# Delta rule's triangular inverse: transpose by 128x128 TensorE transposes and a ScalarE copy

## The reference

```python
lower = jnp.where(strict, jnp.einsum("nbhid,nbhjd->nbhij", kb, kc) * decay, 0.0)
eye = jnp.eye(c, dtype=F32)
rhs = jnp.concatenate([vc * bc[..., None], kb * jnp.exp(gc)[..., None]], axis=-1)
sol = lax.linalg.triangular_solve(lower + eye, rhs, left_side=True, lower=True)
```

## Time and profile before

| what | us |
|---|---|
| median of 3 runs | 1694.83 |
| lowest and highest | 1693.57 and 1696.85 |
| profiled execution, span | 1692.8 |
| PE busy | 1670.1 |
| DVE busy | 1152.0 |
| ACT busy | 968.3 |

### The profile page before, as it was taken

One profiled execution on the slowest core, in us unless ns is written; L12 is line 12 of the kernel. 1 busy time (PEld: TensorE's weight loads), 2 busy tenths in 40 slices (PEclk: granted clock), 3 DMA queues, 4 the chain that ended last, 5 costly groups with the idle time before them and its releaser, 6 DMA issues.

```text
span 1692.8 us, 24538 instructions
## 1 busy us (share of the span) xinstructions
PE 1670.1 (99%) x10066; PEld 1383.8 (82%) x10066; DVE 1152.0 (68%) x1835; ACT 968.3 (57%) x1522; POOL 19.9 (1%) x54
## 2 busy tenths in 40 slices
PE   9999999999999999999999999999999999999998
PEld 7778888887888888888888888888888888888886
DVE  6887875778788667555676578655575556985554
ACT  7845554577374447444667676544464456975443
POOL 1000000010000000000000000000000000000000
PEclk9999999999999999999999999999999999999999
DMA  7323355542244555455544335555555555455553
GB/s 265 125 82 132 147 183 187 178 169 107 77 168 162 180 196 188 178 195 177 210 185 153 134 124 177 218 194 190 208 192 194 181 217 187 149 187 180 193 180 143
DMA packets 41872, 291.67 MB, mean 172 GB/s; under 512 B 4673, under 2 KB 4929, under 8 KB 7713
## 3 DMA queue, kind: packets, MB, share of 16 engines
q1 hardware_dynamic: 39312, 280.68, 46.0%
q0 software_dynamic: 2304, 8.91, 1.5%
q10 hardware_dynamic: 144, 0.52, 0.1%
HBM read 289.05 MB, written 1.05 MB: 171 GB/s over the span
## 4 chain that ended last, share of the span: by engine, by line
PE 84%; DVE 10%; ACT 3%; issue 1%; DMA 1%; SPq 0%; DVEq 0%; ACTq 0%
PE pg L535 21%; PE pg L538 21%; PE pg L536 21%; PE pg L485 4%; PE pg L487 3%; PE pg L486 3%; DVE wl L2004 3%; PE ps L843 2%; PE ps L678 2%; DMA raw<-weights 1%; ACT wh L1339 1%; PE ps L892 1%; PE ps L662 1%; PE ps L964 0%; DVE hTl L2603 0%
## 5 line engine op out<-in xcount | busy, mean ns | idle before, releaser
L2004 DVE TENSOR_TENSOR wl<-raw,wh 128x1024 fp32r<-128x1024 f32 x494 | 581.3, 1220 | 183.7 <-ACT wh L1339 180.6
L535 PE MATMUL pg<-wh,hTh 128*128 128x512 f32 x1676 | 661.0, 394 | 1.3 <-ACT arena L1391 1.0
L538 PE MATMUL pg<-wh,hTl 128*128 128x512 f32 x1676 | 653.4, 390 | 0.0
L536 PE MATMUL pg<-wl,hTh 128*128 128x512 f32 x1676 | 652.5, 389 | 0.0
L1339 ACT ACTIVATE wh<-raw 128x1024 fp32r<-128x1024 f32 x522 | 522.8, 1054 | 201.7 <-DMA raw<-weights 191.4
L538 PEld LDWEIGHTS pg<-wh,hTl 128*128 128x128 f32 x1676 | 314.5, 188 | 67.0 <-DVE hTl L2070 0.3
L535 PEld LDWEIGHTS pg<-wh,hTh 128*128 128x128 f32 x1676 | 314.8, 188 | 64.0 <-ACT arena L1391 1.4
L536 PEld LDWEIGHTS pg<-wl,hTh 128*128 128x128 f32 x1676 | 315.0, 188 | 62.2
L485 PE MATMUL pg<-wh,hTh 128*128 128x512 f32 x416 | 171.4, 412 | 2.2 <-DVE wl L2004 2.2
L1445 ACT ACTIVATE arena<-pg,sm 128x256 f32<-128x256 f32 (+1 forms) x67 | 36.6, 547 | 237.4 <-PE pg L538 237.3
L487 PE MATMUL pg<-wh,hTl 128*128 128x512 f32 x416 | 163.0, 392 | 0.0
(11 more groups left out here) (406 smaller groups left out, 1322.7 us busy)
## 6 DMA issues: line engine op xcount, KB each, us to landing
raw<-weights SPq DMA_DIRECT2D x265, 1024.0 KB, 4.8
arena<-wide POOLq DMA_DIRECT2D x9, 512.0 KB, 3.7
raw<-weights SPq DMA_DIRECT2D x2, 512.0 KB, 6.4
cst<-const_tables POOLq DMA_DIRECT2D x1, 1024.0 KB, 5.3
plainh<-dist_tables POOLq DMA_DIRECT2D x2, 512.0 KB, 6.2
arena<-gate_mix POOLq DMA_DIRECT2D x1, 1024.0 KB, 8.3
x<-x_in ACTq DMA_DIRECT2D x1, 512.0 KB, 3.9
x<-x_in SPq DMA_DIRECT2D x1, 512.0 KB, 9.5
```

The source lines that it names most:

```text
L535: pe.matmul(dst, high, wh[:, slot, at], start=start, stop=False)
L536: pe.matmul(dst, high, wl[:, slot, at], start=False, stop=False)
L538: return pe.matmul(dst, low, wh[:, slot, at], start=False, stop=stop)
L2004: tt(wl[:, slot, h], raw[:, slot, h], wh[:, slot, h], ALU.subtract)\
```

## The change

Products are still 64x64, but the transpose of X is no longer updated beside X. In each level PE does the first block, then transposes all of X with eight full 128x128 transposes into banks 2 and 3, then `prepare(1)`; ACT copies the 128x1024 result to `XT_` (a new wait `inv_w` on ACT and `inv_w_read` on PE); PE then does one block of 32 products for X's new term. A 128x128 transpose of a pair of chunks also swaps which row half a chunk's block lies in, so all products now run between the two row halves, in quarters (0,0), (1,1), (1,0), (0,1), and the bank goes by the half that is read. The third block, DVE's addition to the transpose (L2292), the copy to `LT`, the second transposes at L858, the separate start of `XT_` (L2261, L2268, L2270) and ACT's copies at the end (L1559) go. The last level is like the others. DVE writes all finished matrices with eight additions of 64x256 after one wait, two of them before `inv_scaled`'s first signal and six before its second. The masks of a level become 128 wide: the constants hold 5 masks of 64 and 6 of 128 columns instead of 12 of 64, 320 columns more in the same DMA.

```diff
-MASK_NAMES = ("eye", "up", "lo", "ups", "los", "nlo1", "nlo2", "nlo4", "nlo8", "nlo16", "nlo32", "nup1")
+MASK_NAMES = ("eye", "up", "lo", "ups", "los")
+STEPS = (1, 2, 4, 8, 16, 32)
...
-    for s in (1, 2, 4, 8, 16, 32):
-        c[f"nlo{s}"] = -1.0 * ((q // (2 * s) == g // (2 * s)) & (q // s > g // s))
-    c["nup1"] = -1.0 * ((q // 2 == g // 2) & (q < g))
-    main = np.concatenate([np.asarray(c[n], np.float32) for n in CONST_NAMES + MASK_NAMES], 1)
+    for s in STEPS:
+        same_pair = q // (2 * s) == g // (2 * s)
+        c[f"step{s}"] = np.concatenate([-1.0 * (same_pair & (q // s < g // s)), -1.0 * (same_pair & (q // s > g // s))], 1)
+    names = CONST_NAMES + MASK_NAMES + tuple(f"step{s}" for s in STEPS)
...
+        STEP_MASK = {s: cst[:, at + i * P:at + (i + 1) * P] for i, s in enumerate(STEPS)}
+        at += len(STEPS) * P
...
+        def halves(ap, last=False):
+            return ap.rearrange("p (q m f) -> p q m f" if last else "p (m q f) -> p m q f", m=M, f=CHUNK)
...
-                L4, LT4, X4, XT4, T4 = (blocks(v) for v in (Lm, LT, X_, XT_, TM_))
+                L4 = blocks(Lm)
+                inverse, turned, term = halves(X_, True), halves(XT_, True), halves(TM_)
...
-                def natural(v):
-                    return lambda d, h, m, a: v[a, 4 * d + h, m, :]
-                def paired(v):
-                    return lambda d, h, m, a: v[a, 4 * (h // 2) + 2 * d + h % 2, m, :]
-                def block_products(bank, ds, lhs, rhs, from_home, to_home, done, move=None):
-                    for d in ds:
-                        for h in range(2):
-                            for m in range(M):
-                                for g in range(2):
-                                    for r in range(2):
-                                        a, b = (half(r if home or not g else 1 - r) for home in (from_home, to_home))
-                                        at, i = (2 * d + h) * M + m, (d, 2 * g + h, m, a)
-                                        out_ = ps[b, bank + g, at * CHUNK:(at + 1) * CHUNK]
-                                        if move and g:
-                                            pe.matmul(out_, ident[a, a], move(*i), start=True, stop=False)
-                                        last = pe.matmul(out_, lhs(*i), rhs(*i), start=not (move and g), stop=True)
-                    last.then_inc(sem[done], 1)
+                def place(q):
+                    return slice(q * CHUNK, (q + 1) * CHUNK)
...
-                                last = pe.matmul(ps[half(r), d, (h * M + m) * CHUNK:(h * M + m + 1) * CHUNK],
+                                last = pe.matmul(ps[half(r), m, place(2 * h + d)],
                                                  L4[half(r), 4 * d + h, m, :], ident[half(r), half(r)],
                                                  start=True, stop=True)
-                                if h >= 2:
-                                    at = (2 * d + h - 2) * M + m
-                                    low, unit = L4[half(r), 4 * d + h, m, :], ident[half(r), half(r)]
-                                    last = pe.matmul(ps[half(1 - r), 2, at * CHUNK:(at + 1) * CHUNK],
-                                                     unit if d else low, low if d else unit, start=True, stop=True)
                 last.then_inc(sem["low_t"], 1)
                 prepare(4)
-                inverse, turned, term = paired(X4), paired(XT4), paired(T4)
-                lower = [natural(LT4), natural(L4)]
-                for i, s in enumerate((2, 4, 8, 16, 32)):
-                    t = 2 * (i % 2)
+                for s in STEPS[1:]:
+                    out_bank = 2 if s == STEPS[-1] else 0
                     c.wait("inv_x")
-                    block_products(t, (0, 1), lambda d, *at: lower[d](d, *at), inverse, True, False, "inv_t")
+                    for h in range(NH):
+                        for d in range(2):
+                            for r, m in ((0, 0), (1, 1), (1, 0), (0, 1)):
+                                last = pe.matmul(ps[half(m), r, place(2 * h + d)], L4[half(r), 4 * d + h, m, :],
+                                                 inverse[half(r), 2 * h + d, m, :], start=True, stop=True)
+                    last.then_inc(sem["inv_t"], 1)
+                    for q in range(2 * NH):
+                        last = pe.transpose(ps[:, 2 + q // NH, (q % NH) * P:(q % NH + 1) * P], X_[:, q * P:(q + 1) * P], ident)
+                    last.then_inc(sem["inv_w"], 1)
                     prepare(1)
+                    c.wait("inv_w_read")
                     c.wait("inv_tm")
-                    block_products(2 - t, (0, 1) if s < 32 else (1,), turned, term, False, True, "inv_y")
-                    block_products(t, (0, 1) if s < 32 else (0,), term, turned, False, s == 32, "inv_yt",
-                                   turned if s == 32 else None)
+                    for h in range(NH):
+                        for d in range(2):
+                            for r, m in ((0, 0), (1, 1), (1, 0), (0, 1)):
+                                last = pe.matmul(ps[half(r), out_bank + m, place(2 * h + d)],
+                                                 turned[half(m), 2 * h + d, r, :], term[half(m), r, 2 * h + d, :],
+                                                 start=True, stop=True)
+                    last.then_inc(sem["inv_y"], 1)
                     prepare(1)
 
                 c.wait("inv_scaled")
...
-                c.wait("low_t")
-                c.wait("sc_masked")
-                for d in range(2):
-                    act.activation(LT[:, 512 * d:512 * d + 512], ps[:, d, :], ACT.Copy).then_inc(sem["low_t_read"], 1)
                 prepare(4)
                 act.activation(DELTA_Z, DELTA_Z, ACT.Silu).then_inc(sem["delta_z_ready"], 1)
                 c.wait("norms_ready")
                 for level in range(5):
+                    c.wait("inv_w")
+                    act.activation(XT_, ps[:, 2:4, :].rearrange("p b n -> p (b n)"), ACT.Copy)\
+                       .then_inc(sem["inv_w_read"], 1)
...
-                c.wait("inv_yt", 5)
-                new = ps[:, 1, 0:256].rearrange("p (h m f) -> p m h f", m=M, f=CHUNK)
-                for m in range(M):
-                    for r in range(2):
-                        dst, _ = diagonal(2 * m + r)
-                        last = act.activation(dst[half(r), 2:4, half(r)], new[half(r), m], ACT.Copy)
-                last.then_inc(sem["inv_copied"], 1)
...
-                X5, XT5 = (v.rearrange("p (g d q f) -> p g d q f", g=2, d=2, f=CHUNK) for v in (X_, XT_))
-                L5, LT5 = (v.rearrange("p (d g q f) -> p g d q f", g=2, d=2, f=CHUNK) for v in (Lm, LT))
-                def pair_mask(name):
-                    return MASK[name].unsqueeze(1).unsqueeze(1).broadcast_to([P, 2, 4, CHUNK])
+                T8 = TM_.rearrange("p (k e) -> p k e", e=P)
+                inverse, product = halves(X_, True).rearrange("p q m f -> p m q f"), halves(ps[:, 0:2, :].rearrange("p b n -> p (b n)"))
+                first, first_product = (v.rearrange("p m (h d) f -> p d m h f", d=2) for v in (inverse, product))
 
                 c.wait("low_t")
-                tt(XT3[:, 8:16, :], ps[:, 2, :].rearrange("p (q f) -> p q f", f=CHUNK), times(MASK["nup1"], 8), ALU.mult)
-                c.wait("low_t_read", 2)
-                for d, A in enumerate((L5, LT5)):
-                    last = tt(X5[:, :, d], A[:, :, d], pair_mask("nlo1"), ALU.mult)
+                for d in range(2):
+                    mask = STEP_MASK[1][:, d * CHUNK:(d + 1) * CHUNK].unsqueeze(1).unsqueeze(1)
+                    last = tt(first[:, d], first_product[:, d], mask.broadcast_to([P, M, NH, CHUNK]), ALU.mult)
                 c.step(last)
                 c.sig(tt(X3, X3, times(MASK["eye"], 16), ALU.add), "inv_x")
-                for d, AT in enumerate((LT5, L5)):
-                    last = tt(XT5[:, 0, d], AT[:, 0, d], times(MASK["nup1"], 4), ALU.mult)
-                c.step(last)
-                c.step(tt(XT3, XT3, times(MASK["eye"], 16), ALU.add))
                 prepare(4, 0)
                 for i, s in enumerate((2, 4, 8, 16, 32)):
-                    t = 2 * (i % 2)
-                    x_term, xt_term = (ps[:, b:b + 2, :].rearrange("p b (q f) -> p (b q) f", f=CHUNK) for b in (2 - t, t))
                     c.wait("inv_t")
-                    c.sig(tt(T3, xt_term, times(MASK[f"nlo{s}"], 16), ALU.mult), "inv_tm")
+                    c.sig(tt(T8, ps[:, 0:2, :].rearrange("p b (k e) -> p (b k) e", e=P), times(STEP_MASK[s], 8),
+                             ALU.mult), "inv_tm")
...
-                        c.sig(tt(X3, X3, x_term, ALU.add), "inv_x")
-                        c.wait("inv_yt")
-                        c.step(tt(XT3, XT3, xt_term, ALU.add))
+                        c.sig(tt(inverse, inverse, product, ALU.add), "inv_x")
...
-                        old, new = (v.rearrange("p g (h m f) -> p m g h f", m=M, f=CHUNK)
```

(25 more changed lines are left out.)

12 lines of the change are left out of this document (6 added, 6 removed).

## The result

The changed kernel takes 1682.93 us (median of 4 runs, 1682.77 to 1683.70), the kernel before on the same chip 1694.74 (4 runs, 1693.57 to 1696.85). The ratio is 0.9931 [0.9919, 0.9944], faster by 0.7%. Its profiled span is 1681.0 us against 1692.8: 11.8 less, where 11.4 was forecast.

A forecast was written before the change was run, and what follows sets the result against it. PE's own queue was taken as the bound, with DVE leading before the first level. Per layer 4.89 + 0.61 - 0.40 = 5.10, twice 10.20, plus 1.60 (stop), less 0.40 (table): 11.4 off 1694.8 gives 1683.4 us, range 1680.0 to 1689.0.

The forecast's parts named there:

- The level: Each inverse level on PE: two blocks, transposes and two filler pieces take 6.17 us in place of 7.22.
- stops of the old stretch: PE's levels: the rest of 4.89 us saved per layer, beyond 1.05 in each of four levels.
- ACT's copy: Between transposes and second block: hidden by filler, no cost, margin 0.17 us; 0.3 late once per layer, taken as nothing.
- DVE's addition: X's addition before the next level's first block: done at 6.1 us, PE comes at 6.17; no cost, margin 0.1.
- Start of X: Before the first level: L2261 leaves DVE's chain, so the level starts 0.61 us sooner in each layer.
- End of the last level: Before the scan's first state product: DVE's eight writes and L2332 make PE stop 0.4 us per layer.
- The table: Constants' DMA: 320 more columns, 164 KB, delay the weight unit's landing on the chain by 0.4 us, once.
- The stop: Second layer, second level's last block: the unnamed PE stop goes as runs of 128 become 64, saving 1.60 us.
- banks apart: Rival: separate banks speed blocks to 0.93 us against 1.10, twenty blocks save 3.4, giving 1680.0; chance 0.06.
- products don't overlap: Rival: blocks between row halves take 1.84 us, 29 ns an instruction, giving 1698.3, slower; chance 0.05.
- time given back: Rival: PE is relieved but time returns where DVE leads, behind the scan or in front; about 1693, chance 0.05.
- The clock: Rival: PE's clock falls to 1.2 GHz in the levels, doubling 58.5 us of both layers to 1742; chance 0.01.

The follow-up runs named there:

- The larger table: Changed kernel with 1280 unread columns of zeros (0.66 MB) added to the table of constants: 1684.59 us.
- the new writes: Changed kernel with DVE making only two of the last level's eight writes, then one addition to X, and ACT copying the other six tiles: 1682.61 us.
- both edits again: Second run of the changed kernel with the new writes and half of a weight unit's split moved behind the first X: 1681.59 us.
- the runs of 192: Changed kernel with an unread third block and both filler pieces before the second block, making runs of 192 short products: 1699.0 us.
- the version with the banks: Changed kernel with the second block's products of both row halves sent to one bank and DVE adding to X in four instructions: 1693.08 us, one run.

## Why the prediction was right

It gave 1683.4 for 1682.93, by way of a span 11.4 shorter, and 11.8 was measured. The terms did not all come as taken: the levels gave 0.4 less than 9.78 + 1.60 (4.57 + 6.45), the new stops cost 0.3 less than 0.80, the start of X gave 0.1 more than 1.22, and the table, which was to cost 0.40, cost 0.05 in this pair of profiles. These errors partly cancel. The steps one by one:

- **The level.** 6.17 predicted, 6.18 measured. The block took 1.10 and the third block of before was worth some 1.85, shown by putting it back. The transposes took 0.85 from first start to next start, where 0.79 was taken from the earlier trace rows; the pieces of filler took 1.56 and 1.58 where 1.59 was. These two errors cancel. A part of the gain, 1.0 us in a layer, was not the block but PE's two stops for DVE in the old levels, which the prediction counted in its 4.89 as "stops of the old stretch". The stretches are 29.58 and 29.34 for 29.26, the 0.3 of the first being mostly the slower block in the third level (0.24).
- **ACT's copy.** 1.03, where two smaller ones (1.09) had been taken for it. It cost nothing, and the margin of 0.17 was about right (0.2). Without the filler it costs 1.1 a level. The prediction had it 0.3 late once in a layer, behind the full third level; it was not late there (1.13 after the first transpose, as elsewhere).
- **DVE's addition.** It ended at 100.70 with PE's next block at 100.86. The margin of 0.1 was 0.16. That it was the next limit is shown by the version with four additions: every level stopped for what they took more.
- **Start of X.** 0.61 was taken. Measured from the landing's end, so without what the landing adds, the first level of the first layer starts 0.61 sooner (60.87 to 60.26); by the clock of the profile it is 0.56. The second layer gained 0.72 up to there. PE still waits there for DVE (0.31 and 0.61).
- **End of the last level.** A new stop of 0.40 was forecast and one of 0.25 came, in the place and behind the instruction named. DVE's first four writes took 1.74 and the next four 1.61, against the 1.70 each that were assumed, and L2299 ended at 122.20. PE came at 3.94 from the blocks' end in both.
- **The table.** 0.4 was taken. All profiles together give some 0.4 of landing time, the first pair 0.24, and in that pair only 0.05 reached the levels. The larger table shows that the term exists at all. It is smaller than what one execution differs from the next by.
- **The stop.** That it would go was right: no `issue` wait stands in the profile after. The reason was wrong. The prediction tied it to the run of 128 instructions. A stop of a microsecond didn't come back with runs of 128 or of 192, and it did in the kernel before, at the same instruction. It is the prediction's one step whose mechanism failed, and it carried 1.60 of 11.4. That moving the code was enough to be rid of it was luck; in its place the first block of the first layer's third level lost 0.24. The prediction also said that nothing in the trace tells its cause. "What holds PE at that instruction" below shows what does.

Of the rivals, "banks apart" falls, "products don't overlap" is shown to be what a different order of the same loops gives, and "time given back" falls by the list of places. The clock stayed at 1.00 over the stretches with the transposes. The Trainium skill, TensorE: Matmul & The Clock Gate, Part 4, says that transposes do not count as busy for the clock; with eight transposes in 6.2 us beside full products no row here shows it, and longer runs of them were not tried.

**What holds PE at that instruction.** No engine is named, and nothing to speak of moves on the DMA engines during the stop (kernel before, columns as in the earlier trace rows with all of PE's loads: length, busy, clock, DMA share, GB/s):

```profile
419.40:420.80 1.40, 0.04 (x1) 1.00 0.00 0
```

But just ahead of it one packet of a DMA queue for instructions lands. The row of this queue (packets, MB, share of 16 engines' time) in the stretch from 418.1 to 419.5 of the kernel before, then from 417.5 to 418.9 of its second profile:

```profile
q8 instruction: 1, 0.02, 5.1%
```

```profile
q8 instruction: 1, 0.02, 4.4%
```

In the first the packet runs from 418.22 to 419.37 and PE goes on at 420.82, 1.45 after its end; in the second from 417.82 to 418.79 and PE goes on at 420.24, again 1.45 after its end. The packet comes 0.33 sooner against the block's start, and the stop is 0.34 shorter. The smaller delays fit in: in the slow block of the third level PE goes on 1.42, 1.43, 1.48 and 1.50 us after the end of such a packet (the changed kernel twice, the new writes, both edits again), in the two stops of the runs of 192 after 1.39 and 1.33, and in two stops inside the filler of the version with the banks after 1.32 and 1.34. The queue is PE's by its count: 79 packets for PE's 20132 instructions before, 75 for 19076 after, 80 for 20356 with the third block, some 254 or 255 instructions a packet. The slow block goes on at PE's 1711th recorded instruction in all four profiles, and with runs of 192 at the 1967th, which is 256 later.

So the stop is, as far as traces can say, PE waiting for its next packet of instructions. The place is set by the count of instructions, and the length by when the packet arrives. No run delayed or hastened a packet on purpose, so this is read from the traces and not shown by an experiment. **What stays open** is why the packet comes late at these places and in time at the others.

## What to carry to other kernels

Count small products by the quarter of the array that each uses, in order. Four in turn took 17 ns each and two in turn 29, and the order of one loop decided between 0.7% faster and 0.2% slower. A new copy on another engine costs nothing only while a piece of independent work lies between the block that makes its input and the block that reads its output: compare the two times to a tenth of a microsecond, and look at the engine that comes next (here DVE, done 0.16 ahead of PE's need). When a term of a forecast is a stop without a named cause, price it by itself, profile the kernel before twice to see whether it belongs to a place, and look at the packets of the instruction queues just ahead of it. And take a difference between two profiles by place only after taking off what an early landing adds: here it moved everything behind it by up to 0.8 us from one execution to the next.

## What the runs showed of the hardware that was not expected

**The clock fell for some 3 us in five of the fourteen profiles, and it cost time in at least one of them.** Stretch 74.0 to 75.5 of the changed kernel, then of the kernel before (columns as in the stretches above):

```profile
74.00:75.50 1.50, 1.50 (x6) 1.21 (x5) 1.47 (x2) 1.47 (x3) 0.00 (x0) 0.50 0.00 0
```

```profile
74.00:75.50 1.50, 1.50 (x8) 1.26 (x7) 1.47 (x2) 1.47 (x3) 0.00 (x0) 1.00 0.00 0
```

0.50 is 1.2 GHz. It fell between 72 and 73 (mean 0.61), when PE was in a row of 96 short instructions (L820 and L829, 68.96 to 73.98), and was back behind 76. The second profile of the changed kernel doesn't have it, so it isn't the change's doing. PE came to the transposes of L at 80.43 instead of 79.38, but it had to wait for DVE in front of the first level in any case, and it cost nothing. The version with the banks has it in the same place (mean 0.68 over 71 to 76), the third block put back has it behind the same lines in the second layer (0.81 over 390 to 395), and so has the second profile of both edits (0.50 over 384 to 386). The larger table's profile has it at another place:

```profile
36.00:37.00 1.00, 1.00 (x4) 0.81 (x3) 0.96 (x3) 0.85 (x1) 0.00 (x0) 0.50 0.00 0
```

There PE had stood idle for DVE, for 1.92 us before 34.52. Its matmuls then start 0.43 apart in place of 0.23 from 35.88 to 38.87, and the chain runs through them. From the landing's end to the first level that is the 61.39 in place of 60.26 to 60.31, some 1.1 us.

**A third of the transposes of L went and none of their time.** They were 96 instructions of 64x64, 64 of them at L852 and 32 at L858, which used the other quarters in between, and took 2.01 us together (79.38 to the next start at 81.39). The 64 that are left, in two quarters, take 2.01 (80.43 to 82.44), 31 ns each. PE's timeline of the changed kernel:

```profile
80.43 2.08 PE L843 MATMUL ps<-cst,arena 64*64 64x64 f32 x64
```

It is the same effect of the quarters, and it costs nothing here, since this too lies ahead of the wait for DVE.

**A change between 64-row and 128-row products seems to have a price.** In a piece of filler behind a short block the second matmul starts 0.33 after the first and the others 0.23 after one another (99.28, 99.61, 99.84 in the second level of the changed kernel), and the short block behind the piece starts 0.32 after its last matmul (97.86 to 98.18). That is some 0.1 for each change. With the filler in one place instead of two, the same instructions took 7.61 to 7.67 us in five levels of eight (7.82 in one, and 8.2 in the two with a stop), instead of 8.04. That is more than two such changes, and it was not taken apart further.
